# A decoder layer on one core: the first norm's squares added on VectorE, tables loaded behind the input, earlier sums and roots, and the last norm on 128x4 values

## The chip, the core and the metric

One NeuronCore of a Trainium2 chip runs the whole layer. Its engines are TensorE (PE in the profile, weight loads as PEld), VectorE (DVE), ScalarE (ACT), GpSimd (POOL) and SyncE (SP, which here only issues transfers). Each engine runs its own list of instructions in order; they meet through semaphores. The metric is the device time of one execution in microseconds (us), lower is better.

## The reference, cut to what matters

One layer on x of 1024 tokens by 1024 features: a SwiGLU block, two kinds of windowed attention merged by gates, a second SwiGLU block, and a last norm.

```python
def rms_norm(x, g):
    y = x32 * lax.rsqrt(jnp.mean(x32 * x32, axis=-1, keepdims=True) + EPS)
    return (y * g).astype(x.dtype)

h = x + 0.5 * swiglu(rms_norm(x, ffn1_norm), ...)            # block 0
u = rms_norm(h, mix_norm)
h = h + merged_attention(u) @ w_out
h = h + 0.5 * swiglu(rms_norm(h, ffn2_norm), ...)            # block 1
return rms_norm(h, final_norm)
```

There are four norms. The kernel numbers them 0 to 3: norm 0 stands before block 0, norm 1 before the attention, norm 2 before block 1, and norm 3 is the last one.

## The kernel before, in words

Everything is kept transposed: features on the 128 partitions, in 8 tiles k (`KT`), and the 1024 tokens in the free dimension, in two halves of 512 (`hf`, `HALF`). `h` holds the residual. Every product in float32 accuracy is made of three float32r products: a number is split into a high part (ACT, a copy that rounds) and a low part (DVE, the difference), and PE multiplies high by high, low by high and high by low (`triple` L1921 to L1923, `product` L1877 to L1879). Weight tiles are `op_h`/`op_l` in 6 slots, the moving operands of a block are `B11`, `B21` (half 0) and `B12`, `B22` (half 1; `B12` lies in `T4`'s place and the profile calls it `T_h`/`T_l` there).

**A block** (`ffn(f)`, f = 0 or 1) is a fixed list of 158 + 77 steps. Every engine has its own loop over the same step numbers, and numbers in those loops decide what stands where. The first 32 steps are plain products: step s takes one weight tile through 4 triples (12 matmuls). Steps 0 to 3 need half 0 of the input, steps 4 to 7 half 1. The moving operands of the plain steps are not normalised: the norm's factor `rstd` is applied to the products afterwards on DVE (`scaled_gate`, `scaled_up`), so PE can start before the norm is known.

**A norm** goes through four engines: ACT squares the 8 tiles of a half (`square`, L909) into two buffers `sq`, POOL adds them into `acc` (`add_squares`, L779), PE multiplies `acc` by a matrix `ones` of 1/1024 and so sums over the partitions into a PSUM bank, the same sum on all partitions (`sum_squares`, L1903), ACT takes the root (`root_of`, L921) and DVE the reciprocal on 128x512 values (`invert`, L1285). `LATE` says how many of the last squares skip POOL's adds and go to PE one by one (L1906): two, for norm 3, half 1. For norms 0 and 2 PE's sums stand at steps 5 and 10 and DVE's reciprocals at steps 6 and 12.

**The start.** SP issues the input in 8 transfers of two tiles (`x_in[0]` to `x_in[3]` are half 0), with the first weights between them. POOL issues four tables: `tab` and `hot` for the attention's distance biases, `bias_in` and `sink`. ACT and DVE split tile 0 and 1 (`raw_high`, `raw_low`), then weight tile 0, then tiles 2 to 7, then weight tiles 1 to 3. PE's small products `hot` by `tab` (`distance_biases`, L1914) stand before step 2. ACT copies their result into `rows`, and POOL writes those to memory.

**The end.** After the last product, norm 3 of half 1 is all that is left. Result tiles are `hg`: n counts them in the order of `K_ORDER[1]` = (4, 5, 6, 7, 0, 1, 2, 3). DVE makes n = 0 to 4 (`result`, L1544); for n = 5 to 7 ACT multiplies `h` by the gain (L915) and POOL by `rstd` (L864). SP writes them out in the order of `RESULT_ORDER`, waiting for each in turn (L754).

## Time and profile before

| what | value |
|---|---|
| median of 3 runs | 2081.93 us (2081.64 to 2082.69) |
| the profiled execution | 2082.57 us, span in the profile 2080.4 us |
| busy | PE 98%, PEld 79%, DVE 67%, ACT 38%, POOL 9% |
| mean granted TensorE clock | 0.993 |

The span is the time from the first to the last instruction, 2.2 us less than the time of that execution. The page also cuts the span into 40 equal slices of 52 us: PE is busy for 90% or more of 38 of them, for 80 to 90% of the first and 60 to 70% of the last. A chain of waits follows the end of the program back to what released each step. In a row of the timeline or the chain the first number is the start, the second the duration, both in us.

### The profile page before, as it was taken

To read this page: it belongs to the slowest core of one execution; us is meant where nothing else is said; L and a number is where in the kernel's file an instruction comes from. 1 tells how busy PE (TensorE), PEld (TensorE's weight loads), DVE (VectorE), ACT (ScalarE), POOL (GpSimd) and SP (SyncE) were. 2 spreads that over 40 slices of the span, in tenths; PEclk is the share of its full clock that TensorE was granted. 3 is DMA by queue.
4 is the path that set the end of the run, shared out by engine and by line. 5 is a ranking of instruction groups with operands and counts; after the bars stand their busy time and mean duration, and the time that the engine had idled before them with its cause. 6 is when DMAs were issued, how large, how long until landed. Compare 5 with 4: busy or idle time off the path is not lost.

```text
span 2080.4 us, 26482 instructions
## 1 busy us (share of the span) xinstructions
PE 2032.7 (98%) x9404; PEld 1650.4 (79%) x9404; DVE 1394.8 (67%) x2317; ACT 795.8 (38%) x1495; POOL 182.2 (9%) x160
## 2 busy tenths in 40 slices
PE   8999999999999999999998999999999999999996
PEld 5878888888887777777776888887878888888884
DVE  4987666666988455566775443458876676667976
ACT  6342333334455243443545112134433323334453
POOL 4000000000022000142440000012000000000012
PEclk9999999999999999999999999999999999999998
DMA  5232333257446111001114111123233323267433
GB/s 177 81 101 102 106 107 106 87 193 253 162 127 202 37 41 41 31 31 42 45 47 147 46 51 50 51 82 117 79 119 112 101 97 107 99 210 248 137 101 107
DMA packets 85803, 217.40 MB, mean 105 GB/s; under 512 B 9195, under 2 KB 9231, under 8 KB 83888
## 3 DMA queue, kind: packets, MB, share of 16 engines
q1 hardware_dynamic: 69568, 164.66, 23.5%
q10 hardware_dynamic: 14480, 46.16, 6.2%
q0 software_dynamic: 1632, 4.98, 0.7%
q8 instruction: 73, 1.20, 0.2%
q14 instruction: 50, 0.41, 0.1%
HBM read 160.68 MB, written 55.08 MB: 104 GB/s over the span
## 4 chain that ended last, share of the span: by engine, by line
PE 90%; DVE 6%; issue 1%; ACT 1%; DMA 1%; POOL 0%; DVEq 0%; ACTq 0%; SPq 0%; POOLq 0%
PE bank L1921 20%; PE bank L1923 19%; PE bank L1922 19%; PE bank L1877 9%; PE bank L1878 9%; PE bank L1879 9%; PE bank L2072 1%; PE bank L2109 1%; PE bank L2085 1%; DVE op_l L1342 1%; PE bank L2141 0%; DVE B_l L1307 0%; DVE B_l L1336 0%; DMA h<-xT 0%; PE bank L2122 0%
## 5 line engine op out<-in xcount | busy, mean ns | idle before, releaser
L1921 PE MATMUL bank<-B_h,op_h 128*128 128x512 f32 x624 | 247.7, 397 | 10.6 <-DVE op_l L1342 9.1
L1877 PE MATMUL bank<-xh,wh 128*128 128x512 f32 x640 | 257.0, 402 | 0.0
L1921 PE MATMUL bank<-T_h,op_h 128*128 128x512 f32 x640 | 249.2, 389 | 1.9 <-DVE U L1433 1.9
L1878 PE MATMUL bank<-xl,wh 128*128 128x512 f32 x640 | 250.2, 391 | 0.0
L1879 PE MATMUL bank<-xh,wl 128*128 128x512 f32 x640 | 250.1, 391 | 0.0
L1923 PE MATMUL bank<-T_h,op_l 128*128 128x512 f32 x640 | 249.0, 389 | 0.0
L1922 PE MATMUL bank<-T_l,op_h 128*128 128x512 f32 x640 | 249.0, 389 | 0.0
L1922 PE MATMUL bank<-B_l,op_h 128*128 128x512 f32 x624 | 245.1, 393 | 0.0
L1923 PE MATMUL bank<-B_h,op_l 128*128 128x512 f32 x624 | 245.0, 393 | 0.0
L1921 PE MATMUL bank<-gs_h,op_h 128*128 128x512 f32 x616 | 240.5, 390 | 0.7 <-DVE gs_l L1376 0.7
L1923 PE MATMUL bank<-gs_h,op_l 128*128 128x512 f32 x616 | 239.7, 389 | 0.0
L1922 PE MATMUL bank<-gs_l,op_h 128*128 128x512 f32 x616 | 239.7, 389 | 0.0
L947 ACT ACTIVATE op_h<-S 128x512 fp32r<-128x512 f32 x144 | 90.7, 630 | 214.5 <-PE bank L1923 171.9
L1342 DVE TENSOR_TENSOR op_l<-S,op_h 128x512 fp32r<-128x512 f32 x144 | 98.9, 687 | 84.1 <-ACT op_h L947 84.1
L1877 PEld LDWEIGHTS bank<-xh,wh 128*128 128x128 f32 x640 | 120.5, 188 | 37.1 <-issue 10.6
L1921 PEld LDWEIGHTS bank<-B_h,op_h 128*128 128x128 f32 x624 | 118.5, 190 | 38.8 <-DVE op_l L1342 10.0
L947 ACT ACTIVATE op_h<-A 128x512 fp32r<-128x512 f32 x132 | 83.3, 631 | 153.7 <-PE bank L1923 153.7
L1921 PEld LDWEIGHTS bank<-T_h,op_h 128*128 128x128 f32 x640 | 120.1, 188 | 27.7 <-DVE U L1433 2.8
L1342 DVE TENSOR_TENSOR op_l<-A,op_h 128x512 fp32r<-128x512 f32 x132 | 93.0, 704 | 73.1 <-ACT op_h L947 73.0
L1879 PEld LDWEIGHTS bank<-xh,wl 128*128 128x128 f32 x640 | 120.4, 188 | 25.9
L1922 PEld LDWEIGHTS bank<-T_l,op_h 128*128 128x128 f32 x640 | 120.2, 188 | 25.0
L1878 PEld LDWEIGHTS bank<-xl,wh 128*128 128x128 f32 x640 | 120.7, 189 | 24.2 <-issue 0.7
(198 smaller groups left out, 3549.7 us busy)
## 6 DMA issues: line engine op xcount, KB each, us to landing
gr<-g_ops SPq DMA_DIRECT2D x154, 256.0 KB, 2.7
raw<-stream SPq DMA_DIRECT2D x56, 512.0 KB, 3.4
gate<-ffn_in SPq DMA_DIRECT2D x44, 512.0 KB, 4.0
up<-ffn_in SPq DMA_DIRECT2D x44, 512.0 KB, 4.9
g_ops<-tT SPq DMA_DIRECT2D x78, 256.0 KB, 2.0
g_ops<-gb SPq DMA_DIRECT2D x58, 256.0 KB, 5.0
A<-ffn_down ACTq DMA_DIRECT2D x6, 1536.0 KB, 7.7
h_spill<-h ACTq DMA_DIRECT2D x32, 256.0 KB, 2.4
```

Source lines behind the costliest of these rows:

```text
L947: nc.scalar.activation(op_h[(o + W_TURN[f]) % W_SLOTS][:], operand(o), ACT.Copy).then_inc(op_high, 1)
L1342: nc.vector.tensor_tensor(op_l[slot][:], operand(o), op_h[slot][:], ALU.subtract).then_inc(op_low, 1)
L1877: nc.tensor.matmul(out, wh[slot][:, cols], hi, start=first, stop=False)
L1878: nc.tensor.matmul(out, wh[slot][:, cols], lo, start=False, stop=False)
L1879: return nc.tensor.matmul(out, wl[slot][:, cols], hi, start=False, stop=last)
L1921: nc.tensor.matmul(out, op_h[slot][:, cols], hi, start=first, stop=False, skip_group_check=True)
L1922: nc.tensor.matmul(out, op_h[slot][:, cols], lo, start=False, stop=False, skip_group_check=True)
L1923: return nc.tensor.matmul(out, op_l[slot][:, cols], hi, start=False, stop=last, skip_group_check=True)
L2072: last = nc.tensor.matmul(bank[2 + i // 2][:, i % 2 * 2 * P + lo:(i % 2 + 1) * 2 * P], q[part, tile * P:(tile + 1) * P], k[part, (tile - 1 ...
L2085: last = nc.tensor.transpose(bank[4 + i // 2][:, (i % 2 * 2 + b) * P:(i % 2 * 2 + b + 1) * P], sp[c % 3][:, i, b * P:(b + 1) * P], ident[:])
L2109: last = nc.tensor.matmul(bank[6][a * HD:(a + 1) * HD, to:to + width], values[:, tile, a * HD:(a + 1) * HD], moving, start=first, stop=fir ...
```

## The change

1. POOL makes a second constant, EPS/1024^2, and issues only `tab` at once. `hot` waits for the last transfer of half 0 (`x_in[3]`), `bias_in` and `sink` for the last of half 1 (`x_in[7]`). PE's products of `hot` and `tab` stand before step 4.
2. The squares of norm 0 are added by DVE, not by POOL: 7 adds for each half, after the weight tiles that it splits anyway.
3. Weight tile 0 is split after tile 0 of the input, not after tile 1.
4. Sums and reciprocals stand sooner: block 0 at steps 5, 8 and 6, 9; block 1 at 3, 5 and 4, 6.
5. Norm 3, half 1: four squares (n = 4 to 7) have buffers of their own and go to PE alone. PE uses the squares as weights and one column of `ones` as the moving operand, so that the sums come out as 128 tokens on the partitions by 4 values. Root (ACT) and reciprocal (DVE) are taken on 128x4 values; DVE spreads them on the diagonals of `diag`, and PE multiplies `ones` by it twice, into banks 1 and 2. DVE reads the factor from bank 1 for n = 0 to 5; ACT copies bank 2 to `rstd`, and POOL multiplies n = 6 and 7.

```diff
-LATE = {..., (3, 0): 0, (3, 1): 2}
+LATE = {..., (3, 0): 0, (3, 1): 4}
+SUM_AT = ((5, 8), (3, 5))
+INVERT_AT = ((6, 9), (4, 6))
-DVE_HALF_1 = 5
-RESULT_ORDER = [(0, k) for k in range(KT)] + [(1, k) for k in (4, 5, 6, 1, 7, 2, 0, 3)]
+DVE_HALF_1 = 6
+RESULT_ORDER = [(0, k) for k in range(KT)] + [(1, k) for k in (4, 5, 6, 2, 7, 3, 0, 1)]
...
 (GpSimd)
-            nc.gpsimd.memset(eps[:], EPS).then_inc(made, 1)
+            nc.gpsimd.memset(eps[:, 1:2], EPS / D_MODEL ** 2).then_inc(eps_made, 1)
+            pool.wait_ge(eps_made, 1)
+            nc.gpsimd.memset(eps[:, 0:1], EPS).then_inc(made, 1)
             pool.dma_start(tab[0:N_BUCKETS, :], rel_bias).then_inc(tab_in, 16)
...
+            pool.wait_ge(x_in[3], 16)
+            pool.dma_start(hot[:], onehot).then_inc(tab_in, 16)
+            pool.wait_ge(x_in[7], 16)
+            pool.dma_start(bias_in[:], b_in).then_inc(const_in, 16)
+            pool.dma_start(sink[:], sinks.partition_broadcast(P)).then_inc(const_in, 16)
-            add_squares(0, 0)
-            add_squares(0, 1)
...
-            pool.wait_ge(rstd_done, 8)
+            pool.wait_ge(rstd_copied, 1)
 (ScalarE)
+                alone = n >= KT - LATE[(norm, hf)]
-                if n >= 2:
+                if n >= 2 and not alone:
                     act.wait_ge(sq_sum, base + max(1, n - 2))
...
-                    if j in (5, 10):
-                        root_of(2 * f, j // 10)
+                    if j in SUM_AT[f]:
+                        root_of(2 * f, SUM_AT[f].index(j))
...
-                            root_of(3, 1)
+                            for n in range(DVE_HALF_1, KT):
+                                k = K_ORDER[1][n]
+                                nc.scalar.activation(hg[:, k, HALF:], h[:, k, HALF:], ACT.Copy, scale=gain[:, 3, k:k + 1]).then_inc(x_gain, 1)
+                                if n == DVE_HALF_1:
+                                    act.wait_ge(ssq, 8)
+                                    nc.scalar.activation(root_4[:], bank[0][:, 0:4], ACT.Sqrt, bias=eps[:, 1:2],
+                                                         scale=1.0 / D_MODEL ** 2).then_inc(root, 1)
+                            act.wait_ge(rstd_spread, 2)
+                            nc.scalar.activation(rstd[:, HALF:], bank[2][:], ACT.Copy).then_inc(rstd_copied, 1)
...
 (VectorE; ScalarE's two lines alike)
             raw_low(0, 0, 0)
+            operand_low(0, 0)
             raw_low(0, 0, 1)
-            operand_low(0, 0)
...
+            add_squares(0)
             for k in range(KT):
                 raw_low(0, 1, k)
             for o in range(4, W_SLOTS):
                 operand_low(0, o)
+            add_squares(1)
...
-                    invert(3, 1)
+                    dve.wait_ge(root, 8)
+                    nc.vector.reciprocal(inv_4[:], root_4[:]).then_inc(inv_made, 1)
+                    dve.wait_ge(inv_made, 1)
+                    nc.vector.tensor_tensor(diag[:], ident[:].unsqueeze(1).to_broadcast([P, 4, P]),
+                                            inv_4[:].unsqueeze(2).to_broadcast([P, 4, P]), ALU.mult).then_inc(diag_made, 1)
+                    dve.wait_ge(rstd_spread, 1)
                     for n in range(DVE_HALF_1):
                         result(1, n)
...
-                                               in1=rstd[:, cols], op0=ALU.mult, op1=ALU.mult).then_inc(x_out, 1)
+                                               in1=bank[1][:] if hf else rstd[:, cols], op0=ALU.mult, op1=ALU.mult).then_inc(x_out, 1)
 (TensorE)
+            def last_norm():
+                late = LATE[(3, 1)]
+                pe.wait_ge(sq_sum, adds_before(3, 1) + KT - 1 - late)
+                for n in range(late + 1):
+                    if n:
+                        pe.wait_ge(sq_done, 16 * 3 + 8 + KT - late + n)
+                    squares = late_sq[n - 1] if n else acc[1]
+                    for c in range(4):
+                        last = nc.tensor.matmul(bank[0][:, c:c + 1], squares[:, c * P:(c + 1) * P], ones[:, 0:1],
+                                                start=n == c == 0, stop=n == late, skip_group_check=True)
+                last.then_inc(ssq, 1)
+                pe.wait_ge(diag_made, 1)
+                for b in (1, 2):
+                    nc.tensor.matmul(bank[b][:], ones[:], diag[:].rearrange("p c t -> p (c t)"), start=True, stop=True).then_inc(rstd_spread, 1)
...
-                    if s == 2 and not f:
+                    if s == 4 and not f:
                         distance_biases()
-                    if s in (5, 10):
+                    if s in SUM_AT[f]:
...
-            sum_squares(3, 1)
+            last_norm()
```

How the instructions stand. **GpSimd at the start of the program** (DMA is the issue of a transfer), before:

```order
L760 MEMSET eps_55 128x1
L761 DMA tab_162<-rel_bias 32x20
L762 DMA hot_161<-onehot 33x1536
L763 DMA bias_in_51<-b_in 128x40
L764 DMA sink_54<-sinks 128x8
L765 MEMSET ones_50 128x128
L766 MEMSET ident_49 128x128
```

and now:

```order
L776 MEMSET eps_55 128x1
L777 DMA tab_162<-rel_bias 32x20
L778 MEMSET ones_50 128x128
L779 MEMSET ident_49 128x128
L781 MEMSET tab_162 1x20
L783 ISA
L783 AFFINE_SELECT ident_49<-ident_49 128x128
L786 DMA hot_161<-onehot 33x1536
L788 DMA bias_in_51<-b_in 128x40
L789 DMA sink_54<-sinks 128x8
```

Three of the four table transfers moved behind the small constants, and each of the first two has a wait for input in front of it.

**TensorE at the end of the program** (`op`, `gs` belong to the last product), before:

```order
L1921 MATMUL bank<-gs_h_103_152,op_h_44_93 128x512
L1922 MATMUL bank<-gs_l_107_156,op_h_44_93 128x512
L1923 MATMUL bank<-gs_h_103_152,op_l_50_99 128x512
L1903 MATMUL bank<-acc_118_167,ones_50 128x512
L1906 MATMUL bank<-sq_119_168,ones_50 128x512
L1906 MATMUL bank<-sq_120_169,ones_50 128x512
```

and now:

```order
L1967 MATMUL bank<-gs_h_103_152,op_l_50_99 128x512
L1946 MATMUL bank<-ones_50,acc_118_167 128x1 x4
L1946 MATMUL bank<-ones_50,late_sq_121_170 128x1 x4
L1946 MATMUL bank<-ones_50,late_sq_122_171 128x1 x4
L1946 MATMUL bank<-ones_50,late_sq_123_172 128x1 x4
L1946 MATMUL bank<-ones_50,late_sq_124_173 128x1 x4
L1951 MATMUL bank<-diag_174,ones_50 128x512 x2
```

Three wide products became twenty with one moving column, and two wide ones that wait for DVE.

**VectorE at the end of the program**, before:

```order
L1506 SCALAR_TENSOR_TENSOR h_57<-bank,h_57 128x512 x4
L1544 SCALAR_TENSOR_TENSOR hg_60<-h_57,gain_53,rstd_165 128x512 x2
L1285 RECIPROCAL rstd_165<-rstd_165 128x512
L1544 SCALAR_TENSOR_TENSOR hg_60<-h_57,gain_53,rstd_165 128x512 x5
L443 UNCONDITIONAL_BRANCH
```

and now:

```order
L1532 SCALAR_TENSOR_TENSOR h_57<-bank,h_57 128x512 x4
L1571 SCALAR_TENSOR_TENSOR hg_60<-h_57,gain_53,rstd_165 128x512 x2
L1675 RECIPROCAL inv_126_175<-root_127_176 128x4
L1677 TENSOR_TENSOR diag_174<-ident_49,inv_126_175 128x512
L1571 SCALAR_TENSOR_TENSOR hg_60<-h_57,gain_53,bank 128x512 x6
```

The wide reciprocal gave way to a small one and one multiplication, and the last results, now six, read one operand from a bank.

## Rows read from the trace of the kernel before

**Rows 1.** The page's first part: busy time, share of the span, instructions

```profile
PE 2032.7 (98%) x9404; PEld 1650.4 (79%) x9404; DVE 1394.8 (67%) x2317; ACT 795.8 (38%) x1495; POOL 182.2 (9%) x160
```

**Rows 2.** Chain of waits, 0 to 45 us: start, duration, what

```profile
1.76 8.80 DMA h<-xT
...
11.34 4.16 DVE B_l L1307 x6
15.50 0.61 DVE op_l L1342
...
21.10 2.67 PE bank L1914 x8
```

**Rows 3.** Transfers, 0 to 35 us: queue's packets, MB, share; issue, KB, us to landing

```profile
q0 software_dynamic: 160, 0.23, 4.5%
...
hot<-onehot POOLq DMA_DIRECT2D x1, 198.0 KB, 6.9
```

**Rows 4.** Stretches: length, busy of PE, PEld, DVE, ACT, POOL, granted clock, DMA share, GB/s

```profile
8.00:10.00 2.00, 1.99 (x5) 1.60 (x6) 0.00 (x0) 0.00 (x0) 0.00 (x0) 1.00 1.01 210
10.00:12.00 2.00, 0.94 (x3) 0.21 (x1) 0.66 (x1) 1.36 (x3) 0.00 (x0) 1.00 1.03 406
...
24.00:25.00 1.00, 1.00 (x3) 0.81 (x3) 0.00 (x0) 0.24 (x1) 0.95 (x1) 0.50 0.47 188
```

**Rows 5.** Timeline of DVE at the start: start, us, instruction, idle before and releaser

```profile
26.32 3.78 DVE L1307 SCALAR_TENSOR_TENSOR T_l<-h,gain,T_h 128x512 fp32r<-128x512 f32 x4 [9.01 <-ACT T_h L957]
...
43.30 0.69 DVE L1342 TENSOR_TENSOR op_l<-up,op_h 128x512 fp32r<-128x512 f32 x1 [9.35 <-ACT op_h L947]
```

**Rows 6.** Timelines at the start of block 1, POOL and PE

```profile
1421.67 1.51 POOL L779 TENSOR_TENSOR acc<-acc,sq 128x512 f32<-128x512 f32 x1 [0.85 <-ACT sq L909]
...
1427.70 1.02 PE L1903 MATMUL bank<-acc,ones 128*128 128x512 f32 x2
```

**Rows 7.** Chain of waits at the end, 2055 to 2081 us

```profile
2060.61 1.18 PE bank L1903 x2
2061.78 3.34 PE bank L1906 x4
...
2065.21 0.70 ACT rstd L921
...
2065.93 3.36 DVE rstd L1285
...
2069.39 1.78 DVE hg L1544
...
2072.84 2.99 DVE hg L1544 x3
```

**Rows 8.** Timeline of PE: last product; narrow products, and what follows them

```profile
2057.56 0.39 PE L1923 MATMUL bank<-gs_h,op_l 128*128 128x512 f32 x1
...
1055.04 1.89 PE L2141 MATMUL bank<-ident,wide 128*128 128x64 f32 x16
1056.86 0.93 PE L2072 MATMUL bank<-k,q 64*128 64x128 f32 x8
```

**Rows 9.** Groups by line and shape: count, busy us, mean ns, idle before

```profile
L1739 DVE RECIPROCAL rden<-den 128x4 f32<-128x4 f32 x40 | 6.9, 171 | 0.6
...
L1213 ACT ACTIVATE gate_bias<-bias_in 128x4 f32 x2 | 0.4, 187 | 0.0
```

**Rows 10.** Timelines at the end: DVE and POOL side by side

```profile
2055.94 2.73 DVE L1506 SCALAR_TENSOR_TENSOR h<-bank,h 128x512 f32<-128x512 f32 x4
2058.59 2.42 DVE L1544 SCALAR_TENSOR_TENSOR hg<-h,gain,rstd 128x512 f32<-128x512 f32 x2
...
2057.38 3.08 POOL L779 TENSOR_TENSOR acc<-acc,sq 128x512 f32<-128x512 f32 x2 [12.61 <-ACT sq L909]
2069.36 4.60 POOL L864 TENSOR_TENSOR hg<-hg,rstd 128x512 f32<-128x512 f32 x3 [8.91 <-DVE rstd L1285]
```

**Rows 11.** SP's last issue of an output transfer

```profile
2076.98 0.65 SPq L754 DMA_DIRECT2D outT<-hg  x1
```

61 lines of the change are left out of this document (32 added, 29 removed).

## The prediction

> **What bounds the kernel now.** The page comes first: PE is busy for 2032.7 us of a span of 2080.4 [rows 1]. So most of the span can only be shortened by giving PE less work, and this change gives it none of that. What is to be had lies in the 48 us in which PE isn't busy, and the chain of waits shows where the larger pieces are: the first 16 us and the last 23.
>
> At the start PE waits for data. The second input transfer (tiles 2 and 3 of half 0) is issued at 1.76 us and takes 8.80, to 10.56. DVE then splits tiles 2 to 7 until 15.50 and weight tile 1 until 16.11, and from there PE runs without waiting [rows 2]. So PE's steady work begins 5.6 us after that transfer lands. The reader is to see in the stretches that the queues were busy but slow shortly before: 210 GB/s in 8 to 10 us at a share of 1.01, and 406 GB/s in 10 to 12 at 1.03 [rows 4]. Queue q0, POOL's, moved 0.23 MB in 160 packets and yet took 4.5% of 35 us, 1.57 us of all 16 engines [rows 3].
>
> At the end PE has nothing but the norm. The last product starts at 2057.56 and gives way 0.23 us later, at 2057.79 [rows 8]. POOL's last add ends at 2060.46 [rows 10], the sums of `acc` and of two squares run to 2065.13, then root, reciprocal (3.36 us) and five results to 2075.83 [rows 7]. SP issues its last transfer at 2076.98 [rows 11], and the program ends at 2080.4, 4.57 us after DVE's last result.
>
> **The start, part by part.** *Tables later (1).* I read the loss of rate as the small pieces of POOL's tables. Lower value: the bytes missing in 8 to 10 us, (406-210) x 2 = 392 KB, are 0.97 us at 406 GB/s. Upper value: all of q0's 1.57 us. Only what was served before 10.56 us counts, so I take 1.3 us. The bound from the other side is 0, if the rate was low for another reason; a loss would need a table that PE has to wait for, which is a rival below. DVE's splits of tiles 2 to 7 take 0.69 us each (six in 4.16 [rows 2]) and follow the landing, so the 5.6 us stay and PE's steady work starts 1.3 us sooner.
>
> *Products of the tables before step 4, not 2.* They take the same 2.67 us [rows 2]. After them PE's granted clock fell: it was 0.50 in the stretches of 24 to 27 us, of which one stands in [rows 4]; PE had done nothing but these narrow products since 21.10. Three us at half clock cost 1.5 us. I expect that again two steps later: 0. If the clock doesn't fall it is -1.5, if it falls for twice as long +1.5. PE reaches them at about 16.1-1.3+5.0+5.5 = 25 us (step 1 in 5.0, as from 16.11 to 21.10, steps 2 and 3 in 12 products of 0.23 each).
>
> *DVE adds the squares (2).* 14 adds at about 0.69 us, DVE's time for an instruction of this size, are 9.7 us. They lie in DVE's idle time of 9.01 us before 26.32 and 9.35 before 43.30 [rows 5]; POOL is relieved of them. ACT's squares wait for these adds, two buffers behind, and an add of POOL took up to 1.51 [rows 6]. So ACT is through sooner: adds from about 16 to 22 us, the first four tiles of half 1 split by 25, and PE wants them after the table products, at about 28. On the path: 0. Without this cover each late microsecond would count in full.
>
> *Weight tile 0 sooner (3).* PE could start its first two triples about 0.4 us sooner, and then waits for the same second transfer: 0.
>
> *Sums and roots sooner (4).* The products of `acc` cost the same wherever they stand. In block 1 PE meets the second sum at step 5 as it met the first, 1427.70, and POOL's last add ended at 1423.18 [rows 6]: 4.5 us to spare. The first sum is met two steps of 2.73 us earlier, at 1422.2. Its adds stand before those of the second in POOL's list, and the last residual sum, for which PE waits there too, is done before POOL's last add starts, 1421.67. DVE's reciprocals delay splits that PE uses five steps later: 0. POOL's queue of writes and skewed loads in block 0 starts sooner or at the same time: 0.
>
> **The end.** All times are those of the profile before.
>
> *Sums.* Twenty products of one column each show as two passes each, as float32 products do here [rows 7], so 40 passes. Nearest row: 16 passes with a full 128x128 weight tile and 64 columns, 1055.04 to 1056.86, 0.114 us each [rows 8]. 40 x 0.114 = 4.6 us from 2057.79: 2062.4. With fewer columns it may be less, but the last square is only ready at about 2059.4 (DVE's last sum of h ends at 2058.67 [rows 10], and ACT's square takes 0.63), and eight passes follow: no sooner than 2060.3. Before, PE's four passes of L1906 took 3.34 us [rows 7], twice the 0.43 of a pass at full clock, since PE had idled. If the clock falls near the end here too, as I expect, 0.5 us come on top: 2062.9. If every pass runs at half clock, 40 x 0.23: 2066.9. Against 2065.13 I take -2.2 us, with ends of -4.8 and +1.8.
>
> *Root to factor.* Before: 4.26 us, from 2065.13 to 2069.39. Now root 0.19 and reciprocal 0.17 [rows 9], `diag` 0.69, the first wide product 1.67 at half clock (two passes of L1906) with its load 0.2, and five handovers of 0.06: 3.2 us. -1.05; at full clock -1.9.
>
> *Results.* DVE's results would start at 2066.1. POOL's two need the second wide product (1.7) and ACT's copy (0.7), so they start at 2068.6 and end, at 1.28 each alone, at 2071.2. DVE's six end before that: 6 x 0.68 = 4.1, at 2070.2. Here a row decides. DVE's results ran beside POOL's before and took 1.78 us for the first [rows 7], while its four sums of a bank and h took 0.68 each (2.73 in all) though POOL's adds ran from 2057.38 [rows 10]; the new results read a bank too, so 0.68 is taken. If they were held up as before, the last two would take 1.7 each, ending at 2072.1, 0.9 us later. The Trainium skill ("SBUF — State Buffer", section "Who interferes with whom") says that a DVE instruction with two SBUF inputs contends with a GpSimd instruction that reads SBUF, and that one with at most one SBUF input doesn't. By that rule the factor in a bank saves this 0.9 us; the trace agrees with both halves of it.
>
> From the start of results to the last one it was 6.44 us (2069.39 to 2075.83) and is 5.1: -1.35. SP again has two transfers to issue ahead of the last one, so the 4.57 us stay.
>
> Sum of the end: -2.2-1.05-1.35 = -4.6. With the start's -1.3 it is **-5.9 us**. The profiled execution took 2082.57 us and would take 2076.7; it lies 0.64 above the median, so the forecast for the median is 2081.93-5.9 = **2076.0 us**.
>
> **The rivals.** *A: nothing is won at the start.* The second transfer lands as late as before, because three large transfers share the queues with it. For it: it is one of several in flight. Against it: the rate doubles once the tables are through. Then only -4.6: 2077.3.
>
> *B: slow passes.* PE is at half clock from the first narrow product. For it: PE's clock was down after narrow products at 24 us. Against it: there it fell only when they had all run, not at once. 2066.9 instead of 2062.9, +4.0: 2080.0, no change.
>
> *C, slower: weight load and product don't overlap.* A pass with one column could cost its load and its product one after the other, with 4 sums chained in the same columns of a bank. At p us for a pass the end moves by 40p-5.1; the whole gain of 5.9 is gone at p = 0.28, and from 0.38 the kernel is measurably slower. With 0.39, the whole record of a product in [rows 8], it is 15.6 us: 2076.0+10.5 = 2086.5. Against it: the 0.114 of the same rows, start to start, with loads of just this size.
>
> *D: the table comes late.* `hot` is issued at about 12 us and took 6.9 from issue to landing [rows 3]: 19, against PE's 25. From a landing later than 25 PE stands still, from 31 the gain is gone. For it: POOL issues it while DVE works and the queues are full. Against it: no row shows a POOL transfer of such a size that took twice as long. It gets 4%; at twice the 6.9 us and as much again, a landing at 33, it is 2084. The Trainium skill (the same page, section "SBUF: two separate sides") warns that GpSimd writes the descriptors of transfers that it issues and that DVE in a 2-port mode locks it out meanwhile; that would be such a delay, and no row here shows one.
>
> *E: more than forecast.* Clock dip after the tables gone, or wide products at full clock: -1.5 to -1.75 more, 2074.4.
>
> **Chances.** Forecast 0.57 (2074.8 to 2077.6), A 0.16, B 0.08, C 0.04, D 0.04, E 0.11. A measurement of this kernel can tell about 0.2%, 4.2 us, from no change, so 2077.8 is the limit. Faster: the forecast's 0.57 less 0.03, E, and three quarters of A (0.12): 0.77; I lower it to 0.73, as several small mishaps would each take a part of the 1.8 us of margin. Slower: C and a quarter of D, 0.05. The same: 0.22. The range holds A and E and reaches to B: 2072.6 (E with the sums at their earliest) to 2079.8.
>
> **What would show it.** Start: the second transfer lands near 9.3 us, `hot` near 19, PE without a wait from 14.8, its table products near 25 and a stretch at clock 0.50 behind them. DVE's adds end at about 21.5 and 35. End: 40 passes between the last product and about 2062.9 less 1.3, with 0.11 us between starts; root and reciprocal under 0.2 us each; first wide product done 3.2 us after the sums; six DVE results of 0.68 and POOL last. The prediction is wrong if passes take over 0.2 us, if PE waits anywhere between 15 and 45 us, or if the second transfer lands after 10 us.

## The result, and the profile of the changed kernel

The changed kernel takes 2070.9 us (median of 5 runs, 2069.52 to 2071.82); the kernel before took 2082.3 in the 5 runs beside it. The ratio is 0.9944, with an interval of 0.9933 to 0.9956. Measured again later, beside other kernels, it was 2071.11. The gain is 11.4 us where 5.9 were forecast: the sign was right, and the time lies below the range.

The profiled execution took 2070.9 us, with a span of 2069.1, 11.3 less than before. PE's busy time is 1.7 us more than before; the time in which it isn't busy fell from 47.7 us to 34.7.

```profile
PE 2034.4 (98%) x9442; PEld 1654.8 (80%) x9442; DVE 1397.6 (68%) x2333; ACT 793.4 (38%) x1493; POOL 159.4 (8%) x144
```

The chain of waits at the start, against [rows 2]. The input's second transfer is no longer in it. It runs from the first weight tile's transfer (`gate`) over ACT and DVE to PE at 7.95 us, and stays on PE from there. A piece is from one product's start to the next one's, so the second column shows PE's pace: 0.43 us a product up to 13.44, 0.23 from 13.95.

```profile
1.25 5.27 DMA gate<-ffn_in
6.54 0.64 ACT op_h L957
7.20 0.70 DVE op_l L1368
7.95 0.79 PE bank L1965
8.74 0.43 PE bank L1966
...
13.01 0.43 PE bank L1967
13.44 0.51 PE bank L1965
13.95 0.23 PE bank L1966
...
21.89 2.67 PE bank L1958 x8
24.56 0.43 PE bank L1965
24.99 0.23 PE bank L1966
```

Two lines of PE's timeline serve as marks below: the start of step 1 (PE's second weight tile) and the first sum of norm 0. Before:

```profile
16.16 0.79 PE L1921 MATMUL bank<-B_h,op_h 128*128 128x512 f32 x1 [1.08 <-DVE op_l L1342]
...
33.60 1.02 PE L1903 MATMUL bank<-acc,ones 128*128 128x512 f32 x2
```

and now:

```profile
13.42 0.53 PE L1965 MATMUL bank<-B_h,op_h 128*128 128x512 f32 x1
...
27.35 1.02 PE L1935 MATMUL bank<-acc,ones 128*128 128x512 f32 x2
```

The stretches, against [rows 4] (same columns: length, busy time of PE, PEld, DVE, ACT and POOL with their instructions in brackets, granted clock, DMA share, GB/s). The rate from 8 to 10 us is 405 GB/s where it was 210, and behind the table products the clock is 1.00 where it was 0.50.

```profile
8.00:10.00 2.00, 2.00 (x5) 1.61 (x6) 1.93 (x4) 1.99 (x4) 0.00 (x0) 1.00 1.07 405
10.00:12.00 2.00, 2.00 (x7) 1.51 (x6) 2.00 (x4) 1.98 (x4) 0.56 (x1) 1.00 1.01 385
...
24.00:25.00 1.00, 1.00 (x4) 0.46 (x3) 1.00 (x3) 1.00 (x3) 0.00 (x0) 1.00 0.03 12
```

The timeline at the end (start, duration, instruction, idle before it and its releaser), against [rows 7] and [rows 10]. The last product starts at 2051.30 and gives way at 2051.53.

```profile
2049.69 2.73 DVE L1532 SCALAR_TENSOR_TENSOR h<-bank,h 128x512 f32<-128x512 f32 x4
2050.41 2.67 ACT L921 ACTIVATE late_sq<-h 128x512 f32<-128x512 f32 x4 [8.93 <-DVE h L1532]
...
2051.53 0.95 PE L1946 MATMUL bank<-ones,acc 128*128 128x1 f32 x8
...
2052.34 4.84 PE L1946 MATMUL bank<-ones,late_sq 128*128 128x1 f32 x32
...
2057.21 0.26 ACT L1117 ACTIVATE root<-bank,eps 128x4 f32<-128x4 f32 x1 [3.52 <-PE bank L1946]
...
2058.47 3.48 PE L1951 MATMUL bank<-diag,ones 128*128 128x512 f32 x4 [1.29 <-DVE diag L1677]
...
2060.58 4.04 DVE L1571 SCALAR_TENSOR_TENSOR hg<-h,gain,bank 128x512 f32<-128x512 f32 x6 [2.17 <-PE bank L1951]
2061.98 0.60 ACT L1120 ACTIVATE rstd<-bank 128x512 f32<-128x512 f32 x1 [3.89 <-PE bank L1951]
2062.66 2.49 POOL L879 TENSOR_TENSOR hg<-hg,rstd 128x512 f32<-128x512 f32 x2 [24.14 <-ACT rstd L1120]
```

**Where the 11.3 us come from.** Two marks split the kernel: PE's sum of norm 0, half 0 (the first product of `acc`), and the start of the last product. PE reaches the first at 27.35 us, before at 33.60, 6.25 sooner. It reaches the second at 2051.30, before at 2057.56 [rows 8], 6.26 sooner. So the 2000 us between give nothing in sum. That the two marks agree to 0.01 is partly luck: other profiles with the same instructions in between take 1.1 us less (e10) to 0.6 more (e14) for them, in part because the clock falls to 0.50 at other times. From the last product's giving way to the end of the span it was 22.6 us (2057.79 to 2080.4) and is 17.6: 5.0. The end came out near the forecast's 4.6. The start gave 6.25 where 1.3 was forecast.

### The profile page after: what moved, and what is told of

Read it like the earlier page. It is cut to its first block, busy times and chain, and to the rows that moved or that the text cites. A ratio compares the mean times of both kernels' runs of the same rounds, so it can differ in the third digit from the quotient of the medians.

```text
span 2069.1 us, 26547 instructions
## 1 busy us (share of the span) xinstructions
PE 2034.4 (98%) x9442; PEld 1654.8 (80%) x9442; DVE 1397.6 (68%) x2333; ACT 793.4 (38%) x1493; POOL 159.4 (8%) x144
## 4 chain that ended last, share of the span: by engine, by line
PE 89%; DVE 5%; issue 3%; ACT 1%; DMA 1%; POOL 0%; POOLq 0%; ACTq 0%; DVEq 0%; SPq 0%
PE bank L1965 20%; PE bank L1967 20%; PE bank L1966 20%; PE bank L1911 9%; PE bank L1913 8%; PE bank L1912 8%; PE bank L2154 1%; PE bank L2117 1%; PE bank L2130 1%; PE bank L2186 1%; DVE op_l L1368 0%; PE bank L2167 0%; DMA z_in<-gz 0%; DVE wl L1290 0%; DVE sp L1735 0%
## 5 line engine op out<-in xcount | busy, mean ns | idle before, releaser
L1911 PEld LDWEIGHTS bank<-xh,wh 128*128 128x128 f32 x640 | 120.3, 188 | 36.9 <-issue 10.6
L1965 PEld LDWEIGHTS bank<-T_h,op_h 128*128 128x128 f32 x640 | 120.1, 188 | 28.3 <-DVE U L1459 2.8
L1967 PEld LDWEIGHTS bank<-T_h,op_l 128*128 128x128 f32 x640 | 120.1, 188 | 25.1
L1912 PEld LDWEIGHTS bank<-xl,wh 128*128 128x128 f32 x640 | 120.5, 188 | 24.2 <-issue 0.7
L1966 PEld LDWEIGHTS bank<-T_l,op_h 128*128 128x128 f32 x640 | 120.1, 188 | 24.7
```

Of the source, the lines that this page charges most:

```text
L1911: nc.tensor.matmul(out, wh[slot][:, cols], hi, start=first, stop=False)
L1912: nc.tensor.matmul(out, wh[slot][:, cols], lo, start=False, stop=False)
L1965: nc.tensor.matmul(out, op_h[slot][:, cols], hi, start=first, stop=False, skip_group_check=True)
L1966: nc.tensor.matmul(out, op_h[slot][:, cols], lo, start=False, stop=False, skip_group_check=True)
L1967: return nc.tensor.matmul(out, op_l[slot][:, cols], hi, start=False, stop=last, skip_group_check=True)
```

## The experiments

Theory T: POOL's table transfers held up the input by about 3 us; without them PE's two waits close, and with the waits goes part of the time that PE runs at its lower pace. The rivals: the order of the splits and DVE's adds did it; or it is scatter from one execution to the next.

### The tables back in front, and which of them matters

e1 puts all three behind `tab` again; e2 only `bias_in` and `sink`; e3 only `hot`. Everything else stays as changed. Shown is e1; e2 leaves the two lines of `hot` where they are, e3 those of the other two.

```diff
 (e1_tables_front)
             pool.dma_start(tab[0:N_BUCKETS, :], rel_bias).then_inc(tab_in, 16)
+            pool.dma_start(hot[:], onehot).then_inc(tab_in, 16)
+            pool.dma_start(bias_in[:], b_in).then_inc(const_in, 16)
+            pool.dma_start(sink[:], sinks.partition_broadcast(P)).then_inc(const_in, 16)
...
-            pool.wait_ge(x_in[3], 16)
-            pool.dma_start(hot[:], onehot).then_inc(tab_in, 16)
-            pool.wait_ge(x_in[7], 16)
-            pool.dma_start(bias_in[:], b_in).then_inc(const_in, 16)
-            pool.dma_start(sink[:], sinks.partition_broadcast(P)).then_inc(const_in, 16)
```

> The changed kernel with POOL's three transfers (hot, bias_in, sink) back in front of its list, everything else as changed. Theory T (these transfers slow the input, PE then has two gaps, its clock rises later and falls again after the table products): the second input transfer lands at about 10.5 us instead of by 7.7, PE idles about 1.2 us twice before 16 us, matmuls come to 0.23 us only near 20 us, the first sum stands near 33 us instead of 27.51. Time 2075.5 to 2077.5, that is 5 to 6.4 us above the changed kernel's 2070.9. Rival R1 (the gaps closed because weight tile 0 is split sooner and DVE adds the squares): the gaps stay closed and the time stays within 1.5 us of 2070.9. Rival R2 (only as the prediction had it: the landing moves 1.3 us and nothing follows): 2072.2.

> The changed kernel with only bias_in and sink (about 128 pieces and a broadcast over 128 partitions) back in front; hot stays late. If the small pieces are what slows the input: as with all three in front, some 2075.5 to 2077, second landing near 10.5 us. If it is the bytes of hot: 2071 to 2072, second landing by 8 us.

> The changed kernel with only hot back in front; bias_in and sink stay late. If the small pieces of the other two are what slows the input: 2070.5 to 2072, second landing by 8.2 us, PE without a gap from 8 us on. If hot is the cause: 2074 to 2077 with gaps of about 1 us.

Measured: e1 2074.36 (2072.36 to 2076.45), e2 2075.64 (2073.69 to 2076.79), e3 2072.28 (2071.12 to 2073.2). In ACT's timeline the start of `B_h` behind a transfer tells when that transfer was there. e1:

```profile
10.26 4.04 ACT L965 ACTIVATE B_h<-h,gain 128x512 fp32r<-128x512 f32 x6 [2.90 <-DMA h<-xT]
```

e2:

```profile
8.02 1.33 ACT L966 ACTIVATE B_h<-h,gain 128x512 fp32r<-128x512 f32 x2 [0.61 <-DMA h<-xT]
11.54 2.68 ACT L966 ACTIVATE B_h<-h,gain 128x512 fp32r<-128x512 f32 x4 [2.19 <-DMA h<-xT]
```

e3:

```profile
9.11 3.89 ACT L966 ACTIVATE B_h<-h,gain 128x512 fp32r<-128x512 f32 x6 [1.54 <-DMA h<-xT]
```

In the changed kernel ACT has no such wait behind its first tile at all. So the tables are the cause, and worth 3.4 us here (2074.36 less 2071.0, the mean of the two medians of the changed kernel). That is less than the 5 to 6.4 expected of T alone, so T isn't all. Both kinds of table count: `hot`, 198 KB, delays the second transfer to 9.11, and the other two, 24 KB together, leave the second at 8.02 and delay the third to 11.54. The small ones cost as much as all three (2075.64 against 2074.36, not told apart); in e2's profile the clock also fell to 0.50 within step 1. `hot` alone costs 1.3 by the medians, and the intervals of the ratios overlap (0.9941 to 0.9969, against 0.9933 to 0.9956 of the change).

The trace has more on the small ones. Of the two it is `sink`, 4 KB copied to all partitions. It moves in 16 packets (the pieces that the DMA engines carry) of 256 bytes. In the changed kernel, where it comes late, each took 0.02 us and all 0.3; in e2 the longest took 2.06 us and all 13.1, counted over the DMA engines. `bias_in`'s 16 packets of 1280 bytes took 0.9 us in sum in both. The share of POOL's queue over the first 35 us shows it too. e2:

```profile
q0 software_dynamic: 288, 0.26, 4.9%
```

the changed kernel:

```profile
q0 software_dynamic: 288, 0.26, 2.7%
```

In every profile with `sink` in front its longest packet took 1.6 to 2.1 us. No run moves `sink` alone, so that it does the harm without `bias_in` is read from the packets, not shown by a time.

### The tables alone, in the kernel before

```diff
 (e4_before_tables_late: the kernel before)
-            pool.dma_start(hot[:], onehot).then_inc(tab_in, 16)
-            pool.dma_start(bias_in[:], b_in).then_inc(const_in, 16)
-            pool.dma_start(sink[:], sinks.partition_broadcast(P)).then_inc(const_in, 16)
...
+            pool.wait_ge(x_in[3], 16)
+            pool.dma_start(hot[:], onehot).then_inc(tab_in, 16)
+            pool.wait_ge(x_in[7], 16)
+            pool.dma_start(bias_in[:], b_in).then_inc(const_in, 16)
+            pool.dma_start(sink[:], sinks.partition_broadcast(P)).then_inc(const_in, 16)
             add_squares(0, 0)
             add_squares(0, 1)
```

> The kernel before with only the tables' transfers moved behind the input; nothing else changed, so the table products stand before step 2 and POOL adds norm 0's squares. Theory T: the second transfer lands by 8 us and both gaps of PE close, matmuls at 0.23 us from about 13.5 us: -4.5 to -5 us from that, 2077.5; if the half clock after the table products also goes, as in the changed kernel, -6.4, 2075.9. Rival R1 (splits in another order and DVE's adds are needed for it): -1.3 or less, 2081.

Measured: 2084.47 (2082.95 to 2085.11), against 2081.87 of the kernel before on that chip: slower by 2.6, where a gain of 4.5 was expected. The input did come at 7.47. But POOL's list, in its timeline, now has the wait for the input's last transfer ahead of the first add:

```profile
10.44 0.56 POOL L770 DMA_DIRECT2D hot<-onehot  x1 [7.36 <-DMA h<-xT]
18.43 0.57 POOL L772 DMA_DIRECT2D bias_in<-b_in  x1 [7.44 <-DMA h<-xT]
18.99 0.54 POOL L773 DMA_DIRECT2D sink<-sinks  x1
19.54 1.27 POOL L781 TENSOR_TENSOR acc<-sq,sq 128x512 f32<-128x512 f32 x1
21.62 8.83 POOL L781 TENSOR_TENSOR acc<-acc,sq 128x512 f32<-128x512 f32 x6 [0.81 <-ACT sq L911]
```

ACT is two buffers behind POOL, so it stands for 6.80 us, and the splits of half 1, next in its list, start at 27.82. Beside that, `hot` is missed at step 2, and the clock is at 0.50 from 18.6 to 25.5 us. PE's timeline (three of its waits):

```profile
17.13 1.12 PE L1916 MATMUL bank<-hot,tab 33*4 33x384 f32 x3 [1.08 <-DMA hot<-onehot]
...
29.45 0.47 PE L1923 MATMUL bank<-T_h,op_h 128*128 128x512 f32 x1 [0.72 <-DVE T_l L1309]
31.06 0.50 PE L1923 MATMUL bank<-T_h,op_h 128*128 128x512 f32 x1 [0.67 <-DVE T_l L1309]
```

This is a part of the loss only. The first sum stands at 34.35, 0.75 us later than before, and the last product 3.9 later. Between them lie another wait of 1.11 us, at 56.58, for the root that ACT makes late, and more time at clock 0.50 near 1000 and 1140 us, which no run ties to the tables. The rival of this run, that DVE's adds are needed, was right in the sign.

### DVE's adds: with the late tables, and without them

e7 is the changed kernel with POOL adding norm 0's squares again. e6 is the kernel before with only DVE's adds. e11 is e4 with POOL's adds for half 0 ahead of the wait for `x_in[7]`.

```diff
 (e7_pool_adds: the changed kernel; POOL, then DVE)
+            add_squares(0, 0)
+            add_squares(0, 1)
             pool.wait_ge(vec_out, 4)
...
-            add_squares(0)
...
-            add_squares(1)
```

```diff
 (e6_dve_adds_alone: the kernel before; POOL, then DVE, with the changed kernel's function)
-            add_squares(0, 0)
-            add_squares(0, 1)
...
             for o in range(1, 4):
                 operand_low(0, o)
+            add_squares(0)
...
             for o in range(4, W_SLOTS):
                 operand_low(0, o)
+            add_squares(1)
```

```diff
 (e11_adds_then_tables: e4)
+            add_squares(0, 0)
             pool.wait_ge(x_in[7], 16)
             pool.dma_start(bias_in[:], b_in).then_inc(const_in, 16)
             pool.dma_start(sink[:], sinks.partition_broadcast(P)).then_inc(const_in, 16)
-            add_squares(0, 0)
             add_squares(0, 1)
```

> The changed kernel with POOL adding norm 0's squares again, behind its table transfers; all else as changed. Theory T2 (DVE's adds are what makes the late tables affordable): POOL stands at its wait for the input's last transfer until about 18.5 us, its first add comes at 19.5 instead of DVE's 14.57, ACT's squares wait two buffers behind it and with them ACT's splits of half 1, and PE, which wants these at 24.5 us, waits 3 to 4 us between 24 and 35 us: 2074 to 2075 against 2070.9. Rival (what the prediction had: the adds lie in spare time on either engine, worth 0): 2070.5 to 2071.5, PE without a wait.

> The kernel before with one edit: DVE adds norm 0's squares (after weight tile 3, and after weight tile W_SLOTS-1) and POOL doesn't. Theory: alone it is worth nothing, since PE of the kernel before never waited for half 1's tiles: 2081.5 to 2082.5, first sum near 33.6 us. Rival (the part of the gain at the start that neither the tables nor the last norm explains, some 2 us, comes from these adds): 2079.5 to 2080.5.

> The kernel before with hot behind x_in[3] and bias_in and sink behind x_in[7] as in e4_before_tables_late, but with POOL's adds for half 0 ahead of the wait for x_in[7], so that only the place in POOL's list differs. Theory T2 (what made the late tables dear is POOL's first add standing behind that wait): the first add comes at about 14 us instead of 19.54, ACT is through with half 0's squares 5 us sooner, PE's waits between 28 and 35 us go, and what stays is a wait of 1.1 us for hot at step 2: 2077 to 2079 against 2084.5. Rival (POOL is simply too slow beside DVE and ACT there): 2082 or more.

Measured: e7 2083.01 (2081.86 to 2085.01), 12 us above the changed kernel, and 8 more than expected. e6 2082.21 (2077.31 to 2082.62), ratio to before 0.9995 (0.9986 to 1.0004). Its runs fall in two groups, six from 2082.21 up and five from 2077.31 to 2080.59, all five below the lowest of the 27 runs of the kernel before beside it (2080.83). The profile is of one of these five (2079.43). So the median says 0, and some executions gained 1.4 to 4.7 us; why, isn't shown. e11 2079.65 (2078.79 to 2079.99), 2.4 under before and 4.8 under e4.

In e7 PE reaches its fifth step at 24.2 and finds half 1 unsplit. PE's timeline and two stretches (clock third from the right):

```profile
29.39 0.77 PE L1966 MATMUL bank<-T_h,op_h 128*128 128x512 f32 x1 [5.17 <-DVE T_l L1336]
```

```profile
24.00:29.00 5.00, 0.22 (x1) 0.00 (x0) 0.51 (x1) 3.05 (x6) 4.42 (x5) 0.54 0.00 2
29.00:34.00 5.00, 4.62 (x10) 3.26 (x11) 5.00 (x7) 5.00 (x11) 1.38 (x1) 0.50 0.00 0
```

It waits 5.17 us, runs at half clock for five more, and stands a second time, with 3.8 us from one product's start (43.68) to the next, for the second sum's squares. In the kernel before the same slow adds cost nothing by e6's median, and PE came there 6 us later (30.87 against 24.49). So what the adds are worth hangs on the tables: 0 by the median with them early, 12 us with them late. e11 shows that the place in the list is the reason: the same POOL, the same adds, but the first at 14.67 instead of 19.54, and 4.8 us are back. This is POOL's timeline of e11:

```profile
10.91 0.56 POOL L770 DMA_DIRECT2D hot<-onehot  x1 [7.83 <-DMA h<-xT]
14.67 1.29 POOL L778 TENSOR_TENSOR acc<-sq,sq 128x512 f32<-128x512 f32 x1 [3.19 <-ACT sq L911]
16.76 8.80 POOL L778 TENSOR_TENSOR acc<-acc,sq 128x512 f32<-128x512 f32 x6 [0.80 <-ACT sq L911]
```

### The place of the table products

```diff
 (e5_products_step2: the changed kernel; e8_products_step4_alone: the kernel before, the other way)
-                    if s == 4 and not f:
+                    if s == 2 and not f:
```

e15 is e6 with the products before step 4, e14 is e1 with them before step 2: the same line, edited so.

> The changed kernel with the eight table products before step 2 again. PE would be there at about 16.2 us and hot lands near 17.0: a wait of 0.8 us. Theory T3 (at their new place the products are short of what makes the clock fall, at the old one they follow a slow start): the clock is 0.50 for some 3 us or more behind them, another 1.5 to 3 us: 2073 to 2075. Rival (the fall is a matter of chance from execution to execution, not of the place): 2071 to 2072.

> The kernel before with one edit: the eight table products stand before step 4, not step 2. Theory T3 (narrow products so soon after PE's restart at 16.16 us are what brings the clock to 0.50 behind them; two steps later they don't): no stretch of 0.50 behind them, 1.5 us less, 2080.4, and more executions near the lower end. Rival (the clock's falls there are chance, not place): 2082, and the spread of the runs as before.

> The kernel before with two edits, DVE's adds for norm 0 and the table products before step 4; each alone gave 0. Theory (they work together: the wait of 0.7 us at 27.6 us and the half clock behind it that the products at step 4 had alone go with DVE's adds): 2080 to 2080.5, 2 us below the kernel before. Rival (no interplay): 2082.

> e1_tables_front (2074.36) with the table products before step 2 as well, so DVE's adds, the new order and the new last norm are all that is left of the change. Theory (products at step 4 and DVE's adds only work together: at step 4 PE wants half 1's tiles right behind them, which POOL's adds hold back, and at step 2 the products follow PE's restart): 1.5 to 2 us above e1, 2076 to 2076.5. Rival (the products' place is worth nothing in any company): 2074 to 2075.

Measured: e5 2072.49 (2071.05 to 2073.26), 1.5 above the changed kernel; the intervals of the two ratios overlap. Its profile has the wait for `hot`, 0.78 us, and no fall of the clock, so T3 failed there. e8 2081.99, ratio 1.0 (0.9991 to 1.0009): alone the place is worth nothing. In e8's timeline of PE the reason stands right behind the products, where POOL's adds have held back half 1:

```profile
28.70 0.80 PE L1921 MATMUL bank<-T_h,op_h 128*128 128x512 f32 x1 [0.67 <-DVE T_l L1307]
```

e15, the kernel before with DVE's adds and the products at step 4 together, takes 2080.03, ratio 0.9991 (0.9982 to 1.0), 1.9 us less than before, as expected; that wait is gone. But e6, which differs only in the products' place, has five runs as low, its interval overlaps e15's, and the two profiles reach the first sum together (32.17 and 32.09). So that the two parts only work together isn't shown. e14, e1 with the products back at step 2, takes 2075.19, only 0.8 above e1, between its theory and its rival: with runs from 2072.42 to 2077.88 it settles nothing.

### The order of weight tile 0, and the sums

> The changed kernel with two parts undone: weight tile 0 split after input tile 1 again, and the sums and roots of norms 0 and 2 back before steps 5 and 10. The prediction has 0 for both: within 0.7 us of the changed kernel on the same chip. Rival (they hold part of the 2 us of the start that the tables don't explain): 1 to 2.5 us above it.

> The changed kernel itself on this chip, unedited, as the standard for the other three: 2070 to 2072, first sum at 27.3 to 28 us where PE's clock stays up, 1.5 us later where it falls once in the first 30 us.

```diff
 (e12_order_and_sums_undone: the changed kernel; DVE's two lines alike)
-            operand_high(0, 0)
             raw_high(0, 0, 1)
+            operand_high(0, 0)
...
-SUM_AT = ((5, 8), (3, 5))
-INVERT_AT = ((6, 9), (4, 6))
+SUM_AT = ((5, 10), (5, 10))
+INVERT_AT = ((6, 12), (6, 12))
```

Measured: e12 2071.07 (2070.47 to 2072.77), the changed kernel beside it 2071.11 (2070.01 to 2072.77). Both parts are worth 0, as the prediction had it.

### The end

e9 has everything but the new last norm (the changed kernel with part 5 taken out, so `LATE` 2, `DVE_HALF_1` 5 and the old lines). e10 is the changed kernel with the late squares added in pairs on DVE, so that PE makes 24 passes instead of 40. e13 goes on from there: it sums wide again, and takes the reciprocal root in one ACT instruction.

```diff
 (e9_old_last_norm: the changed kernel)
-            last_norm()
+            sum_squares(3, 1)
...
+                    invert(3, 1)
                     for n in range(DVE_HALF_1):
                         result(1, n)
```

```diff
 (e10_pairs_on_dve: DVE, ahead of its last two results of half 0; PE)
+                    for n in (0, 2):
+                        dve.wait_ge(sq_done, 16 * 3 + 8 + 4 + n + 2)
+                        nc.vector.tensor_tensor(late_sq[n][:], late_sq[n][:], late_sq[n + 1][:], ALU.add).then_inc(paired, 1)
...
-                for n in range(late + 1):
+                for n in range(3):
                     if n:
-                        pe.wait_ge(sq_done, 16 * 3 + 8 + KT - late + n)
-                    squares = late_sq[n - 1] if n else acc[1]
+                        pe.wait_ge(paired, n)
+                    squares = late_sq[2 * n - 2] if n else acc[1]
```

```diff
 (e13_arsqrt: on top of e10. PE, then ACT; the dummy stands ahead of the late squares and loads the table)
+                    last = nc.tensor.matmul(bank[0][:], ones[:], (late_sq[2 * n - 2] if n else acc[1])[:], start=n == 0, stop=n == 2)
...
+                            nc.scalar.activation(root_4[:, 0:1], eps[:, 0:1], ACT.Abs_reciprocal_sqrt)
...
+                            act.wait_ge(ssq, 8)
+                            nc.scalar.activation(bank[1][:], bank[0][:], ACT.Abs_reciprocal_sqrt, bias=eps[:, 0:1]).then_inc(rstd_spread, 1)
+                            nc.scalar.activation(rstd[:, HALF:], bank[0][:], ACT.Abs_reciprocal_sqrt, bias=eps[:, 0:1]).then_inc(rstd_copied, 1)
```

> The changed kernel with the last norm as before (two late squares, four wide passes, root and reciprocal on 128x512, five results on DVE); the start as changed. From the traces the end is worth 5.0 us (22.6 us from the last product's giving way before, 17.6 after), the prediction had 4.6: 2075.9, PE's steady start as in the changed kernel. Rival (the end gained more and the start less than the profiled executions say): 2077 or more.

> The changed kernel with the four late squares added in two pairs on DVE, so that PE makes 24 narrow passes instead of 40; root, reciprocal, diag and spreading as changed. The second pair is added by 2053.86 (two adds of 0.69 from 2052.4), eight passes follow: sums done at 2054.8 to 2055.3 instead of 2057.2 and everything behind it 2 us sooner: 2068.9 against 2070.9. If the clock falls further because PE idles between its passes, each pass behind takes 0.2 us: 2069.7. If DVE's last two results of half 0, now behind the adds, hold up the reciprocal: 0.3 us more.

> A further version of the end: DVE adds the four late squares in two pairs, PE sums acc and the pairs with three wide products (six passes) instead of 40 narrow ones, and ACT makes the factor on 128x512 values in one instruction each for DVE (into a bank) and for POOL, with its table loaded ahead; no reciprocal, no diag, no spreading products. Sums done about 2.9 us after the last product gives way (two DVE adds of 0.69 behind its last sum of h, then two passes), factor 0.7 later, six results of 0.68, 4.5 us to the end: 12.3 us instead of 17.6, so 2065.6. If PE's clock is down or DVE's adds come late: 2067. If ACT's table load is not hidden: 1.3 us more.

Measured: e9 2076.4 (2074.23 to 2077.03), so the new last norm is worth 5.4 (2076.4 less 2071.0), and parts 1 to 4 together 5.9 (2082.25 less 2076.4, same chip). e10 2069.15 (2068.41 to 2070.87), 1.9 less than the changed kernel; its ratio, 0.9941 (0.9928 to 0.9955), isn't told apart from the change's 0.9944, but in its profile the results start 7.06 us after the last product gives way, against 9.05, the 2 us expected. e13 **2065.61** (2065.3 to 2066.09), ratio to before 0.992 (0.9904 to 0.9937): 5.4 us less than the changed kernel and the fastest of all. Its end, in the timeline; PE's last product of block 1 gives way at 2051.58:

```profile
2051.58 1.02 PE L1944 MATMUL bank<-acc,ones 128*128 128x512 f32 x2
2052.39 1.47 DVE L1676 TENSOR_TENSOR late_sq<-late_sq,late_sq 128x512 f32<-128x512 f32 x2
...
2053.12 1.98 PE L1944 MATMUL bank<-late_sq,ones 128*128 128x512 f32 x4 [0.53 <-DVE late_sq L1676]
...
2055.14 0.66 ACT L1119 ACTIVATE bank<-bank,eps 128x512 f32<-128x512 f32 x1 [0.79 <-PE bank L1944]
2055.73 0.68 ACT L1120 ACTIVATE rstd<-bank,eps 128x512 f32<-128x512 f32 x1
2055.84 4.04 DVE L1571 SCALAR_TENSOR_TENSOR hg<-h,gain,bank 128x512 f32<-128x512 f32 x6 [0.66 <-ACT bank L1119]
2056.49 2.50 POOL L880 TENSOR_TENSOR hg<-hg,rstd 128x512 f32<-128x512 f32 x2 [17.93 <-ACT rstd L1120]
```

The results start 4.74 us sooner than in the changed kernel (2060.58), and the factor costs 0.66 us where root, reciprocal, `diag` and the first wide product took 3.4.

### All profiles of the start side by side

From the profiled execution of each kernel. "Waited until" is the end of ACT's wait for an input transfer behind the first; step 1 is PE's second weight tile, 12 products. "Clock up" is the first entry in the trace's record of the granted clock, a rise to 1.00. The views print 1.00 for the time ahead of that entry too, so their column doesn't show the slow start.

| kernel | tables | ACT waited until | step 1 starts | its pace, us a product | clock up | clock at 0.50 later | first sum |
|---|---|---|---|---|---|---|---|
| before | front | 10.59 | 16.16 | 0.43 up to 20.5 | 20.3 | 23.7 to 27.1 | 33.60 |
| e6 | front | 10.91 | 16.43 | 0.43 up to 20.4 | 20.4 | none | 32.17 |
| e15 | front | 10.19 | 15.75 | 0.43 up to 21.0 | 20.9 | none | 32.09 |
| e8 | front | 9.56, 11.78 | 15.97 | 0.23 | 11.2 | 28.3 to 31.7 | 32.26 |
| e1 | front | 10.26 | 15.79 | 0.23 | 15.1 | none | 29.70 |
| e14 | front | 10.38 | 15.85 | 0.23 | 10.6 | none | 29.77 |
| e2 | small in front | 8.02, 11.54 | 15.71 | 0.23, then 0.43 | 13.1 | 16.5 to 19.9 | 31.25 |
| e3 | `hot` in front | 9.11 | 14.59 | 0.23 | 11.8 | none | 28.48 |
| e4 | late | 7.47 | 12.99 | 0.23 | 11.8 | 18.6 to 25.5 | 34.35 |
| e11 | late | 7.94 | 13.54 | 0.23 | 13.9 | 20.7 to 24.1 | 29.87 |
| e7 | late | no wait | 13.05 | 0.23 | 10.8 | 24.4 to 34.7 | 34.85 |
| e9 | late | no wait | 13.18 | 0.23 | 11.1 | 24.7 to 28.1 | 28.68 |
| e12 | late | 7.46 | 13.00 | 0.23 | 10.8 | 24.5 to 27.9 | 28.51 |
| e5 | late | no wait | 13.07 | 0.23 | 11.6 | none | 27.89 |
| e10 | late | no wait | 13.70 | 0.23 | 12.7 | none | 27.62 |
| e13 | late | no wait | 13.20 | 0.23 | 13.6 | none | 27.31 |
| after | late | no wait | 13.42 | 0.23 | 13.5 | none | 27.35 |
| after again (e16) | late | no wait | 13.03 | 0.23 | 12.8 | none | 26.98 |

## Why the prediction missed

**What the profile was read for rightly.** The middle gave nothing in sum, as forecast. (The page has 37 slices at 90% or more, not 38; one in the middle lies between 80 and 90, before and after.) Step 1 starts 5.5 to 5.6 us behind the end of the wait in every kernel of the table whose ACT waited for the second transfer alone (before 5.57, e1 5.53, e3 5.48, e11 5.60): "the 5.6 us stay" held. Weight tile 0 and the sums are worth 0 (e12). `hot` came at 17.0 (issue 10.86 and 6.1 us), well ahead of PE at 21.8. In the results DVE's six took 4.04 us, 0.67 each, while POOL ran its two beside them from 2062.66; with both operands in SBUF, in e9, five took 6.44. That is the rule of the Trainium skill ("SBUF — State Buffer", section "Who interferes with whom"), and this trace agrees with it a second time.

**The step that failed: "so I take 1.3".** Step 1 starts 2.74 us sooner (16.16 to 13.42), not 1.3, and the second transfer landed 2.7 sooner: the trace has it at 10.56 and at 7.87, where 9.3 was forecast. The sum took the bytes missing from 8 to 10 us as a lower value (0.97) and the time of q0's packets on all engines (1.57) as an upper one. Neither is a bound. The kernel waits for a whole transfer, and e2 shows 24 KB setting the third one back from 9.21, its landing in the changed kernel, to 11.52 us. How much of the rate is lost says little about which transfer the loss falls on. Nearly half of the 1.57 us is the 16 packets of `sink`: 12.0 of the 25 us that the queue's packets took in sum. Why they take so long beside the input isn't shown.

**The step that was missing: PE's pace.** In the kernel before, step 1 ran at 0.43 us a product from 16.16 to 20.5. It was in the rows: the chain has 2.67 us of table products at 21.10 and PE starting steadily at 16.11, 5.0 us for 12 products, and the prediction used these 5.0 as the cost of step 1 in the new place, too. In the changed kernel they take 2.87: another 2.0 us. Whoever writes down "12 products in 5.0 us" beside "0.23 each" for the next steps has found a lever, and should ask what the pace hangs on. It is the clock's lower level: in all profiles the trace's record of the clock begins with a rise to 1.00, at 20.3 us before and at 13.5 now, and the products ahead of it come at 0.43 us, those behind it at 0.23. What brings the rise sooner is only in part shown. With the tables late it came between 10.8 and 13.9 us in all ten profiles. With all three in front it came at 20.3 to 20.9 in three (before, e6, e15) and at 10.6 to 15.1 in e1, e8 and e14, though e1's two waits (1.36 and 1.05 us) are much like those of before (1.21 and 1.08). So the waits don't fix it, and how often the 2.0 us are won isn't known. The spread of the runs doesn't tell either: e1's lie 4.1 us apart and the changed kernel's 2.3, but those of the kernel before, beside e1, only 2.6.

**The rival that came true in this profile.** Behind the table products the clock stayed at 1.00, which was part of E, at 0.11: steps 2 to 4, which are the rest up to the first sum, take 8.39 us instead of 9.90, 1.5 less. The change doesn't secure it: e9 and e12 have the products in the same place and fell to 0.50 behind them, the changed kernel in its two profiles, e10 and e13 didn't. The Trainium skill ("TensorE: Matmul & The Clock Gate", section "Part 1: The HAM clock gate") says of PE's slow start that it differs from run to run of one kernel; this case agrees (13.5 and 12.8 us in two profiles of the changed kernel), and here a fall in the middle of the work varies too. 2.74 + 2.0 + 1.5 are the 6.25 us of the start.

By medians the start is worth 5.9 (e9). The tables are worth 3.4 in the changed kernel (e1), and DVE's adds with the products' place 1.9 in the kernel before (e15). These were measured in different company, so they need not add up, and they don't tell how much of each is waiting and how much is the clock.

**"On the path: 0" for DVE's adds** was right for the kernel before, by e6's median, and wrong as a statement on the part. The prediction did see that ACT waits for the adds, and took the cover from the trace of before, where PE came 6 us later. What moving the tables does to POOL's list wasn't asked of the variant that keeps the adds there, and e7 and e4 are the answer: 12.0 and 4.8 (e4 less e11).

**The end, term by term**, from the giving way of the last product.

| term | forecast | measured | from |
|---|---|---|---|
| sums | -2.2 | -1.7 | 7.42 (2057.79 to 2065.21) to 5.68 (2051.53 to 2057.21) |
| root to factor | -1.05 | -0.8 | 4.18 to 3.37 (to 2060.58) |
| results | -1.35 | -1.9 | 6.44 to 4.57 (to 2065.15) |
| last result to the end | 0 | -0.6 | 4.57 to 3.95 |
| sum | -4.6 | -5.0 | |

The mechanism was right and four sizes were off by 0.25 to 0.6, mostly cancelling. The first 29 passes came 0.11 us apart, as forecast, and the last 11, once the clock had fallen, 0.21: 5.7 us where the forecast, with 0.5 for the clock, had 5.1. The stretches show it (20 passes in the 2 us from 2052 on, 11 in those from 2055 on); the clock fell while the weight loads were busy throughout:

```profile
2052.00:2054.00 2.00, 2.00 (x20) 2.00 (x20) 1.74 (x3) 1.65 (x3) 0.00 (x0) 1.00 0.02 8
2055.00:2057.00 2.00, 2.00 (x11) 2.00 (x10) 0.00 (x0) 0.00 (x0) 0.00 (x0) 0.50 0.16 60
```

The agreement of the end with the forecast is in part luck as well. The old end had two lengths: 22.6 us in before, e9, e11 and e15, where the clock was at 0.50 in the wide sums, and 20.9 in e4, e6 and e8, where it fell only behind them. The new one has 16.7 to 17.6. So one pair of profiles can put the new last norm at 3.3 us as well as at 5.0; the medians say 5.4.

Rivals B, C and D did not come: the first passes took 0.11, none near 0.39, and `hot` was in time. A, with nothing won at the start, had 0.16 and missed by the whole of what was found there. The lower end of the range, 2072.6, is called E with the sums at their earliest; by the prediction's own terms that is 2074.4 less 2.6, 2071.8, and the measured 2070.9 lies below that too.

**What stays open.** Whether the fall of the clock can be prevented; what brings its first rise sooner in some executions; why the 16 packets of a 4 KB broadcast take up to 2 us each beside the input; how the 1.9 us of e15 divide between DVE's adds, the wait that goes and the clock, and why five of e6's runs gained as much.

## What to carry to other kernels

A part of a change has no worth of its own: late tables alone cost 2.6 us here (and gained 2.4 where POOL's first adds kept their place ahead of the wait), DVE's adds alone gave nothing by the median, and with each other (and the products' new place) they carried half the gain. Moving a transfer behind a wait moves everything behind it in that engine's list. So cost each part in the company it will have, and ask of each moved wait what stands behind it in its queue.

When the same instruction takes twice as long in one stretch as in the next, that is a term of the sum, however the clock column reads. And a small transfer issued beside the input is priced by the landing that it delays, not by its bytes.

## What the runs showed of the hardware

- Two transfers of 20 and 4 KB beside the input let one of its 512 KB transfers land at 11.52 us (e2) and not at 9.21 (after), and cost the kernel as much as with a third of 198 KB added. The 4 KB one, a copy to all partitions in 16 packets of 256 bytes, took 13.1 us over the DMA engines there, up to 2.06 a packet, and 0.3 in all when it came late.
- In the kernel before, PE's products of 512 columns came 0.43 us apart from the first one, through two waits, up to 20.3 us, where the trace's record of the clock begins with a rise to 1.00. They came at that same pace at 24 to 27 us, where the granted clock was 0.50, the lower level (1.2 GHz); at the upper one they come at 0.23. The clock column reads 1.00 ahead of that first entry all the same.
- At one place of the program, behind the same eight products, the clock fell to 0.50 for about 3.4 us in some executions (e9, e12) and not in others (after, e10, e13), 1.5 us each time.
- Float32 passes with a 128x128 weight tile and one moving column start 0.11 us apart at full clock and 0.21 at half (after).
